# GLA stage: the 16-column decay projection appended to the first head's value tiles, input chunks in the outer loop over four PSUM banks, decay scans head by head

## What is computed

```python
def gla_mixer(x, w_in, w_alpha_up, b_alpha, out_norm, w_out):
    h, dk, dv, c = 4, 128, 256, 64
    proj = x @ w_in
    q, k, v, r, a_low = jnp.split(proj, [512, 1024, 2048, 3072], axis=-1)     # a_low: 16 columns
    log_alpha = log_sigmoid(a_low @ w_alpha_up + b_alpha) / 16
    ...
    cum = jnp.cumsum(to_chunks(log_alpha), axis=3)                            # inside chunks of 64 tokens
    def step(state, inp):
        qi, ki, vi, bi = inp
        q_dec, k_inv = qi * exp(bi), ki * exp(-bi)
        scores = where(causal, q_dec @ k_inv.T, 0)
        o = scores @ vi + q_dec @ state
        k_end = ki * exp(b_last - bi)
        state = state * exp(b_last)[:, None] + k_end.T @ vi
```

## Time and profile before

| | us |
|---|---|
| median of 3 runs (1940.01 to 1941.15) | 1940.86 |
| the profiled execution: its own time | 1938.93 |
| its span, first to last instruction | 1937.1 |
| PE busy (share of the span) | 1878.6 (97%) |
| POOL busy | 916.1 (47%) |
| DVE busy | 833.6 (43%) |
| ACT busy | 706.2 (36%) |
| mean granted clock of PE | 0.984 |

### The profile page before, as it was taken

How to read it: one execution, slowest core, us unless ns; L and a number is a source line. 1 busy time by engine, 2 the same in 40 slices (tenths; PEclk the granted TensorE clock), 3 DMA queues, 4 the chain that set the end, 5 groups by cost and what they waited for, 6 DMA issues and landing times.

```text
span 1937.1 us, 23582 instructions
## 1 busy us (share of the span) xinstructions
PE 1878.6 (97%) x8518; PEld 1503.5 (78%) x8518; DVE 833.6 (43%) x1266; ACT 706.2 (36%) x942; POOL 916.1 (47%) x708
## 2 busy tenths in 40 slices
PE   7999999999999799999999999999999999999998
PEld 6888888786777456878888888877887888888886
DVE  6222235225777743333322222246665465545312
ACT  6444323322222353324443422234434344444321
POOL 4544445485556622544454444543432454444542
PEclk9999999998999899999999999999999999999998
DMA  4332233242221211332222233322221233223331
GB/s 168 108 98 97 95 98 98 95 131 88 82 82 59 83 34 44 98 98 87 98 97 98 90 97 92 101 91 74 88 67 65 88 97 98 94 94 92 100 97 44
DMA packets 52529, 174.54 MB, mean 90 GB/s; under 512 B 6368, under 2 KB 6752, under 8 KB 52464
## 3 DMA queue, kind: packets, MB, share of 16 engines
q1 hardware_dynamic: 52288, 173.37, 28.2%
q10 hardware_dynamic: 176, 0.30, 0.1%
HBM read 166.56 MB, written 2.10 MB: 87 GB/s over the span
## 4 chain that ended last, share of the span: by engine, by line
PE 89%; DVE 6%; ACT 2%; issue 1%; POOL 1%; DMA 1%; SPq 0%; DVEq 0%; ACTq 0%; POOLq 0%
PE acc L1483 27%; PE acc L1485 26%; PE acc L1484 26%; PE acc L1550 1%; PE acc L1552 1%; PE acc L1551 1%; PE acc L1691 1%; PE aux L1667 1%; PE aux L1648 1%; PE aux L1629 1%; ACT w_hi L638 1%; POOL w_lo L557 1%; DVE y_sq L986 1%; PE acc L1777 0%; PE acc L1772 0%
## 5 line engine op out<-in xcount | busy, mean ns | idle before, releaser
L557 POOL TENSOR_TENSOR w_lo<-w_raw,w_hi 128x512 fp32r<-128x512 f32 (+1 forms) x633 | 826.6, 1329 | 981.7 <-ACT w_hi L638 981.6
L1483 PE MATMUL acc<-u_hi,w_lo 128*128 128x512 f32 x1592 | 631.7, 397 | 11.2 <-POOL w_lo L557 8.6
L1484 PE MATMUL acc<-u_lo,w_hi 128*128 128x512 f32 x1592 | 624.1, 392 | 0.0
L1485 PE MATMUL acc<-u_hi,w_hi 128*128 128x512 f32 x1592 | 623.7, 392 | 0.0
L638 ACT ACTIVATE w_hi<-w_raw 128x1024 fp32r<-128x1024 f32 (+1 forms) x317 | 326.7, 1034 | 594.2 <-PE acc L1485 523.9
L1483 PEld LDWEIGHTS acc<-u_hi,w_lo 128*128 128x128 f32 x1592 | 300.5, 189 | 86.4 <-issue 17.1
L1485 PEld LDWEIGHTS acc<-u_hi,w_hi 128*128 128x128 f32 x1592 | 300.3, 189 | 65.5
L1484 PEld LDWEIGHTS acc<-u_lo,w_hi 128*128 128x128 f32 x1592 | 300.7, 189 | 64.0 <-issue 2.0
L1483 PE MATMUL acc<-hid_hi,w_lo 128*128 128x512 f32 x528 | 208.0, 394 | 0.0
L1485 PE MATMUL acc<-hid_hi,w_hi 128*128 128x512 f32 x528 | 207.0, 392 | 0.0
L1484 PE MATMUL acc<-hid_lo,w_hi 128*128 128x512 f32 x528 | 204.9, 388 | 0.0
(11 more groups left out here) (290 smaller groups left out, 2033.5 us busy)
## 6 DMA issues: line engine op xcount, KB each, us to landing
w_raw<-in_w_up SPq DMA_DIRECT2D x132, 512.0 KB, 3.4
w_raw<-in_w_mix SPq DMA_DIRECT2D x69, 512.0 KB, 3.5
w_raw<-in_w_down SPq DMA_DIRECT2D x48, 512.0 KB, 3.5
w_raw<-in_w_gla SPq DMA_DIRECT2D x32, 512.0 KB, 3.4
w_raw<-in_w_down SPq DMA_DIRECT2D x24, 384.0 KB, 3.1
w_raw<-in_w_ple SPq DMA_DIRECT2D x10, 512.0 KB, 3.5
tmp<-tmp SPq DMA_DIRECT2D x36, 64.0 KB, 2.0
h<-in_xT SPq DMA_DIRECT2D x8, 256.0 KB, 6.0
```

The lines of the kernel that those rows point to most:

```text
L557: ins = pool.tensor_tensor(w_lo[:, slot, part], w_raw[:, slot, part], w_hi[:, slot, part].bitcast(F32), ALU.subtract)
L1483: pe.matmul(o, w_lo[:, slot, columns], x_hi, start=first, stop=False)
L1484: pe.matmul(o, w_hi[:, slot, columns], x_lo, start=False, stop=False)
L1485: return pe.matmul(o, w_hi[:, slot, columns], x_hi, start=False, stop=last)
```

## The change

- The 16 columns are appended to the values' 256 of head 0: one step ("gva", 0) with 272-column matmuls, three slabs of 816, 816 and 544 columns in place of one of 128 and two of 1024. The four token tiles have a bank each, and the input chunk is the outer loop (for chunks 0 and 1 the fourth tile comes last). `sums(4)` stands ahead of chunk 6.
- DVE evicts each tile in two pieces, the 16 columns into alow_k (token-major) and the 256 into gvt, with rstd_tok. The diagonals are made between the second and the third tile.
- gk 0 comes right behind. Ahead of its chunk 6, `turn_alow` transposes alow_k into aux bank 3 (DVE copies it to alow_t), and the spread follows. alpha comes after gk 0.
- ACT loads the square root's table ahead of the statistic by a dummy (small[:, 4:5]).
- The scans are steps of their own: cum 0 ahead of gpre 0, cum 1 and 2 behind it, cum 3 behind gv 1. gpre r waits for scan r alone. The temporaries of the decay lie in go, not in tmp.

```diff
-GLA = [("alow",), ("gv", 0), ("alpha",), ("gk", 0), ("cum",), ("gq", 0), ("gpre", 0), ("gv", 1), ("gsc", 0),
+GLA = [("gva", 0), ("gk", 0), ("alpha",), ("gq", 0), ("cum", 0), ("gpre", 0), ("cum", 1), ("cum", 2), ("gv", 1), ("cum", 3), ("gsc", 0),
...
+        al_tmp = [go[:, 2 + c // 2, 2 * (c % 2):2 * (c % 2) + 2, :].rearrange("p a b -> p (a b)") for c in range(G_HEADS)]
...
+            act.activation(small[:, 4:5], eps[:, 0:1], ACT.Sqrt)
             act.wait_ge(ms2_ready, 1)
             act.activation(tok_root, tok_ms, ACT.Sqrt).then_inc(root_ready, 2)
...
-                    act.wait_ge(al_ready, G_HEADS)
+                    act.wait_ge(al_ready, r + 1)
...
-            spread_diag(0, tok_out[:, 0:NT])
-            spread_diag(1, tok_out[:, NT:2 * NT]).then_inc(diag_ready, 1)
-            dve.tensor_copy(rstd_tok[:, :], tok_out[:, 0:NT])
+            link(dve.tensor_copy(rstd_tok[:, :], tok_out[:, 0:NT]))
...
-                if kind == "alow":
-                    dve.tensor_tensor(alow_t[0:G_RANK, :], bank[0:G_RANK, :], rstd[0:G_RANK, :], ALU.mult).then_inc(tile_freed, 1)
+                if kind == "gva":
+                    for tt in range(NT):
+                        bank = acc[:, (t + tt) % BANKS, :]
+                        if tt == 2:
+                            spread_diag(0, tok_out[:, 0:NT])
+                            spread_diag(1, tok_out[:, NT:2 * NT]).then_inc(diag_ready, 1)
+                        dve.wait_ge(tile_done, t + tt + 1)
+                        dve.tensor_scalar(alow_k[:, tt, :], bank[:, G_DV:GVA], rstd_tok[:, tt:tt + 1], None, ALU.mult)
+                        dve.tensor_scalar(gvt[:, 0, tt, :], bank[:, 0:G_DV], rstd_tok[:, tt:tt + 1], None, ALU.mult).then_inc(tile_freed, 1)
+                    dve.wait_ge(alow_turned, 1)
+                    dve.tensor_copy(alow_t[0:G_RANK, :], aux[0:G_RANK, 3, :]).then_inc(alow_ready, 1)
+                    dve.wait_ge(rstd_spread, 3)
+                    link(dve.tensor_copy(rstd[:, :], aux[:, 1, :]))
...
-                    for c in range(G_HEADS):
-                        dve.wait_ge(al_ln, 2 * G_HEADS + c + 1)
-                        link(dve.scalar_tensor_tensor(tmp[:, c, :], gcum[:, c, :], 0.0, tmp[:, c, :], ALU.min, ALU.subtract))
-                        dve.tensor_tensor_scan(gcum[:, c, :], keep[:, :], tmp[:, c, :], 0.0, ALU.mult, ALU.add).then_inc(al_ready, 1)
+                    c = step[1]
+                    dve.wait_ge(al_ln, 2 * G_HEADS + c + 1)
+                    link(dve.scalar_tensor_tensor(al_tmp[c], gcum[:, c, :], 0.0, al_tmp[c], ALU.min, ALU.subtract))
+                    dve.tensor_tensor_scan(gcum[:, c, :], keep[:, :], al_tmp[c], 0.0, ALU.mult, ALU.add).then_inc(al_ready, 1)
...
+            def turn_alow():
+
+                pe.wait_ge(tile_freed, plan.first[("gva", 0)][1] + NT)
+                for tt in range(NT):
+                    last = pe.transpose(aux[0:G_RANK, 3, blk(tt)], alow_k[:, tt, :], ident)
+                last.then_inc(alow_turned, 1)
+                free_when[3] = (alow_ready, 1)
+                spread(4)
...
-                if kind == "alow":
-                    o = free_bank(t)
-                    slabs_ready(n)
-                    for k in range(KD):
-                        pe.wait_ge(u_ready, KD * 4 + k + 1)
-                        last = mm3(o[0:G_RANK, :], (n % RING, slice(k * G_RANK, (k + 1) * G_RANK)), u_hi[:, k, :], u_lo[:, k, :], k == 0, k == KD - 1)
-                    last.then_inc(tile_done, 1)
+                if kind == "gva":
+                    turns = [(k, tt) for k in range(2) for tt in range(NT - 1)] + [(k, NT - 1) for k in range(2)]
+                    for k, tt in turns + [(k, tt) for k in range(2, KD) for tt in range(NT)]:
+                        slot, columns = (n + k // 3) % RING, slice(k % 3 * GVA, (k % 3 + 1) * GVA)
+                        if k == 0:
+                            free_bank(t + tt)
+                        if tt == 0:
+                            slabs_ready(n + k // 3)
+                            if k == 6:
+                                sums(4)
+                            pe.wait_ge(u_ready, KD * 4 + k + 1)
+                        o = acc[:, (t + tt) % BANKS, 0:GVA]
+                        pe.matmul(o, u_lo[:, k, blk(tt)], w_hi[:, slot, columns], start=k == 0, stop=False)
+                        pe.matmul(o, u_hi[:, k, blk(tt)], w_lo[:, slot, columns], start=False, stop=False)
+                        last = pe.matmul(o, u_hi[:, k, blk(tt)], w_hi[:, slot, columns], start=False, stop=k == KD - 1)
+                        if k == KD - 1:
+                            last.then_inc(tile_done, 1)
...
-                    token_tiles(t, n, G_DV, 2, 4, {1: lambda: sums(4), 3: lambda: spread(4)} if step[1] == 0 else None)
+                    token_tiles(t, n, G_DV, 2, 4)
                 elif kind in ("gk", "gq", "gr"):
-                    fm_tile(t, [(n, b) for b in range(KD)], u_hi, u_lo)
+                    fm_tile(t, [(n, b) for b in range(KD)], u_hi, u_lo, None, turn_alow if step == ("gk", 0) else None)
```

More of the change, by code:

```diff
@@ L135 @@
             "aq": (1, 1), "attend": (0, 1), "wa": (1, 2), "ga": (1, 1), "gb": (1, 1), "wb": (1, 1), "wout": (1, 1),
-            "pgate": (1, 1), "pproj": (1, 4), "alow": (1, 1), "alpha": (0, 4), "gk": (1, 1), "gq": (1, 1),
+            "pgate": (1, 1), "pproj": (1, 4), "gva": (3, 4), "alpha": (0, 4), "gk": (1, 1), "gq": (1, 1),
             "gv": (2, 2), "gr": (1, 1), "gout": (0, 2), "gwout": (1, 1)}
@@ L176, in steps @@
             self.tiles += tiles
-            for _ in range(slabs):
+            for i in range(slabs):
                 self.release.append(("tile", self.tiles))
-                self.width.append({"avw": KD * AVW, "alow": KD * G_RANK}.get(step[0], SLAB))
+                self.width.append({"avw": KD * AVW, "gva": min(3, KD - 3 * i) * GVA}.get(step[0], SLAB))
             self.slabs += slabs
@@ L316, in layer_program @@
         dve_step = sem("dve_step")
+        alow_turned = sem("alow_turned")
+        alow_ready = sem("alow_ready")
         gate_act = sem("gate_act")
@@ L530, in _ @@
             gla0 = plan.first["gla"][0]
[L531 to L535, removed]
+            for i in range(3):
+                load(gla0 + i, A["w_gva"][:, 3 * i * GVA:min(3 * i + 3, KD) * GVA])
+            for n in range(gla0 + 3, plan.first["up3"][0]):
+                load(n, A["w_gla"][n - gla0 - 3])
             load_up("up3", A["w_up3"])
@@ L619, in _ @@
             lo_run(at("ple"), at("gla"))
-            lo_part(at("gla") % RING, plan.width[at("gla")], at("gla") + 1)
-            lo_run(at("gla") + 1, at("down3"))
+            for n in range(at("gla"), at("gla") + 3):
+                lo_part(n % RING, plan.width[n], n + 1)
+            lo_run(at("gla") + 3, at("down3"))
             lo_down(at("down3"))
@@ L895, in _ @@
                         act.wait_ge(tile_freed, t + c + 1)
[L896 removed]
+                        act.activation(al_tmp[c], gcum[:, c, :], ACT.Abs).then_inc(al_ln, 1)
                     for c in range(G_HEADS):
                         act.wait_ge(al_ln, c + 1)
[L899 removed]
+                        act.activation(al_tmp[c], al_tmp[c], ACT.Exp, scale=-1.0).then_inc(al_ln, 1)
                     for c in range(G_HEADS):
                         act.wait_ge(al_ln, G_HEADS + c + 1)
[L902 removed]
+                        act.activation(al_tmp[c], al_tmp[c], ACT.Ln, bias=ones[:, 0:1]).then_inc(al_ln, 1)
                 elif kind == "gpre":
                     r = step[1]
[L905 removed]
+                    act.wait_ge(al_ready, r + 1)
                     if r:
@@ L1756, in _ @@
                     pe.wait_ge(gke_ready, r + 1)
-                    pe.wait_ge(tile_freed, plan.first[("gv", r)][1] + 2)
+                    pe.wait_ge(tile_freed, plan.first[("gv", r)][1] + 2 if r else plan.first[("gva", 0)][1] + NT)
                     for c in range(7):
@@ L1868 @@
     gla = []
-    for step in GLA[1:]:
+    for step in GLA:
         if step[0] == "gv":
```

18 lines of the change are left out of this document (9 added, 9 removed).

## The result

| | before | changed |
|---|---|---|
| median, 5 runs each (us) | 1941.03 (1940.01 to 1941.15) | 1930.17 (1929.43 to 1933.28) |
| ratio | | 0.9949, 95% interval 0.9938 to 0.9961 |
| profiled execution, its own time | 1938.93 | 1930.17 |
| its span | 1937.1 | 1928.4 |
| PE / DVE / POOL busy | 1878.6 / 833.6 / 916.1 | 1869.5 / 831.9 / 913.5 |

The account below looks back on a forecast made before the run. PE was taken to bound the kernel, carrying 89% of the chain. Parts 1 and 2 (-6.0), the clock (-1.7) and the stall (+2.1) gave -5.6 us, so 1935.3 us from 1940.86, range 1932.2 to 1939.0.

Parts of the forecast that it names:

- What a matmul costs: PE's start distances: 0.2275 us for 512 columns, 0.120 for 256, hence 0.1267 for 272.
- Rival (c): 272-column matmuls on PE cost as much as 512-column ones: 9.7 us more, +4, 1945 us; chance 0.03.
- Part 1: Projection folded in on PE: 24 matmuls removed, wider ones and four transposes added, net -4.38 us.
- Part 2: Start of the stage: waits of 1.15 us (fourth bank 0.83, sums 0.32) against 2.77 before, -1.62 us.
- Part 3: gk 0 taking the first tile's bank: free just before PE asks, costed at nothing; about 1.1 us without early table load.
- Part 5: Scans head by head: PE stalls in gkv 0 for the mask step, about 1.9 to 2.2 us if the clock held.
- Part 4: Clock fall behind alpha, 1.7 us before: between 1.7 us gained and a second fall, 1.7 us lost.
- The two cases meet: Without the clock's fall -5.6 us, with it -5.9 us, so -5.6 was taken.
- The sum: Whole kernel: -5.6 us, from 1940.86 to 1935.3 us; the forecast's chance 0.74.
- (a): DVE gives more back at three thinly covered joints: gain only 2.8 us, 1938.1 us; chance 0.18 together with (d).
- (b): The rotation over four banks keeps the clock down and makes the kernel slower; chance 0.05.
- (d): The change does nothing: DVE paces the stage's start and removed matmuls become waits; chance 0.18 together with (a).

Follow-up runs that it names:

- e9: The changed kernel without the dummy square root that loads the table ahead of the statistic: 1934.41 us, ratio 0.9970 to the kernel before.
- e0: The kernel before, unchanged, run and profiled again: 1940.41 us, ratio 1.0003.
- e11: The kernel before, unchanged, profiled a third time: 1941.97 us, one run.
- e1: The changed kernel with the four scans back in one piece ahead of gpre 0, the fold kept: 1934.60 us, ratio 0.9966 to the kernel before.
- e4: The changed kernel with scan 3 behind the mask step of head 0 instead of ahead of it: 1932.81 us, ratio 0.9953 to the kernel before.
- e5: The changed kernel with alpha's f32 products over all 128 rows, the 112 added ones zero: 1929.46 us, ratio 0.9941 to the kernel before.
- e3: The changed kernel with the token tile as outer loop, the chunk as inner, sums ahead of the third tile: 1937.85 us, ratio 0.9989 to the kernel before.
- e8: The changed kernel with alpha over 128 rows and scan 3 behind head 0's mask step: 1930.88 us, ratio 0.9957 to the kernel before.
- e6: The changed kernel, unchanged, run and profiled again: 1932.07 us, ratio 0.9958 to the kernel before.

## Why the prediction was right or wrong

- **What a matmul costs: right.** 0.1267 us forecast for 272 columns, 0.126 measured. Rival (c) is out.
- **Part 1, the fold: right.** Transposes 0.44 us (1345.85 to 1346.29; 0.53 forecast). Sums 1.78 us (1336.84 to 1338.62; 1.70 forecast).
- **Part 2, the waits: right.** 0.80 us at the fourth bank (0.83 forecast), 0.31 at the sums (0.32). Parts 1 and 2 together: alpha starts 23.01 us after the stage's first matmul, with gk 0 (5.46 us) now ahead of it; before, 23.41 without. That is 5.86 us won, 6.0 forecast.
- **Part 3, the joint: right.** No wait, 0.16 us of cover; e9 puts the early table at 1.28 us on DVE's side.
- **Part 5, the mask step: place right, size wrong.** It costs 0.61 us (0.33 of it on record as idle) instead of about 2.1. Counted from the stage's start, the last preparation step ended as forecast (1369.3 forecast for a start at 1328.35; 1367.44 for 1326.47). From there to the mask step's end I took 12.3 us and it took 11.02: the step ahead of scan 3 took 1.20 instead of 1.72, the scans' distances were shorter than my sums of durations, and the mask step 2.87 instead of 3.2. PE came 0.36 us later than I had it. I had priced the step ahead of scan 3 and the mask step at their slowest rows.
- **Part 4, the clock, and how the sum uses it: this is the step that failed.** I had the clock's part between 1.7 us gained and 1.7 us lost, from the one fall of one profile, set it against the stall ("The two cases meet"), and carried the difference of one pair of profiles over to the medians. The cases don't meet, since the stall was small. Before lost 1.7, 3.4 and 5.1 us in the stage in its three profiles, of which I had seen the mildest, and the clock of the earlier stage stood in the sum at nothing.
- **The sum.** The changed kernel's profile had no fall, and for that case the forecast was -6.0 - 1.7 + 2.1 = -5.6 us. Measured in the stage: -5.86 for parts 1 and 2, -1.7 for the clock, +0.61 for the stall, +0.11 in gq 0 (1353.11 to 1358.68, 5.57 us, where a tile takes 5.46), together -6.8. So 1.2 of the missing 5.3 us lie in the stage, nearly all in the oversized stall. The other 4.0 lie outside it: 1.9 by the clock ahead of the stage, 2.1 because the profile that I had was quicker than before's median. Without the clock the change is worth 5.1 us. That this is near 5.6 is luck: the 5.6 had 1.7 us of clock in it and 1.5 us of stall too much. Over all runs the kernel before had a mean of 1940.4 us at a mean clock of 0.9840 (59 runs, 54 of them with a clock listed; e0 and e11 not counted), the changed kernel 1931.6 us at 0.9861 (11 runs). 0.0021 of 1940 us is 4.1 us, which leaves 4.7 of the 8.8 us for the change itself.
- **Rivals.** (a) named the right three joints, but they cost 0.80, nothing and 0.61 us, no more than the sum had for them. (b), that the rotation over four banks keeps the clock down and makes the kernel slower, is shown by no run. The rotation ran at 1.00 in four of the eight profiles that have it, and in e1, e4, e5 and e9 the clock fell to 0.50 once in it, from about 14 us after the first u_lo on, in the last quarter of the rotation. e9's PE, in these matmuls:

```profile
1344.28 0.43 PE L1757 MATMUL acc<-w_lo,u_hi 128*128 128x272 f32 x1
1344.51 0.43 PE L1758 MATMUL acc<-w_hi,u_hi 128*128 128x272 f32 x1
```

They lie 0.23 us apart, at a clock of 0.50, instead of 0.126 at 1.00. Such a fall cost 1.7 us, and since e3 without the rotation fell too and was slower, the rotation as its cause is not shown. (d) is out by e1: with the scans in one piece the stage is still 4.9 us shorter, corrected, and some 3.8 by the estimate for full clock.

**What stays open.** In three of three profiles the changed kernel lost nothing in the stage. But e1, e4, e5 and e9, which have its PE program up to alpha (e9 with a later table), all fell at about 14 us from the first u_lo, just behind the sums, while e8, with e5's program up to alpha, did not, and single runs of e6 (1935.02 and 1935.71 us at 0.982 and 0.983) have a clock as low as theirs. So the changed kernel is not immune; how often it falls, and why the same products fall in one execution and not in the next, isn't settled. So it is not shown either that the 1.7 us of clock in the stage are owed to the change.

No version measured beats the changed kernel by more than the intervals; e5, with 128 rows, has the lowest median, 1929.46.

## What to carry to other kernels

Folding 16 columns into a neighbouring projection charged them by width here (0.126 us for 272 columns, 0.120 for 256), instead of at the price of whole matmuls (0.231 us each in the narrow projection), and the input chunk in the outer loop turned waits for its producer into work (3.2 us for u_lo on record in e3, none in the changed kernel). Before summing, look at the granted clock in more than one execution, in the stage and ahead of it: the profile at hand may be a mild one, and here the clock made up about as much of the measured difference as the work did (4.1 and 4.7 us). Take a wait's price from the starts around it: the idle time on record was 0.33 us where the wait cost 0.61. Where the clock slows the waiting engine, the wait that an experiment is to show can be hidden: e9 lost 5.1 us and has no wait at gk 0 where 1.1 us was expected, and in e1 and e4, with as much lost, a wait may be too small or missing for the same reason. A chain on a second engine that is priced operation by operation at the slowest rows can overstate a wait, here 2.1 us for 0.61; take the mixture that the same neighbours gave.

## What was not expected of the hardware

- f32 products with 16 rows were no cheaper than with 128. From alpha's first product to the third matmul behind it: 1349.48 to 1353.68, 4.20 us, with 16 rows; in e5, at the same clock of 1.00, 1354.22 to 1358.11, 3.89 us, with 128. And the clock stayed up behind them in all three profiles with 128 rows.
- In the stage the clock took 0, 1.7, 3.4 or 5.1 us in every one of the fourteen profiles, and two executions of one kernel differed by up to 3.4 us.
- A step on DVE took 0.67 us with GpSimd idle (changed kernel, at 1369.21 us), and 1.20 (changed kernel, 1372.23) or 1.72 (before, 1368.06) while it made low parts; a scan took 1.22 (1369.91) and 2.20 (1373.47) in the two cases, for the same operands.
